# A 31-tap depthwise convolution: its last two channel blocks on TensorE as four stacked, shifted copies and four column groups

## The reference

```python
def mixer_cd(h, w_in, dw_w, dw_b, ln_g, ln_b, sc_w, w_out):
    u = h @ w_in
    v = u[..., :CONF_DIM] * jax.nn.sigmoid(u[..., CONF_DIM:2 * CONF_DIM])
    v = causal_dwconv(v, dw_w) + dw_b            # 31 taps, one filter per channel
    vf = v.astype(jnp.float32)
    mu = jnp.mean(vf, axis=-1, keepdims=True)
    var = jnp.mean(jnp.square(vf - mu), axis=-1, keepdims=True)
    vn = (vf - mu) * lax.rsqrt(var + LN_EPS) * ln_g + ln_b
    conf_out = jax.nn.silu(vn)
    ...                                          # bg * causal_dwconv(cg * hh, sc_w)
    return jnp.concatenate([conf_out, sc_out], axis=-1) @ w_out
```

## Time and profile before

| | us |
|---|---|
| median of three runs | 946.71 (940.55 to 950.35) |
| the profiled execution | 945.4, of which the instructions span 943.7 |
| TensorE busy | 894.6 |
| VectorE busy | 665.2 |
| layer 1's first stage, `gate 0` to the end of `out late` | about 460 to 660 |

### The profile page before, as it was taken

The page is one execution under the profiler, slowest core; times in us unless marked ns, Lnnn a source line. Parts: engine busy times, 40 slices in busy tenths (PEclk is TensorE's granted clock), DMA queues, the critical chain, the costliest instruction groups (busy, mean ns, idle before and its releaser), DMA issues.

```text
span 943.7 us, 17154 instructions
## 1 busy us (share of the span) xinstructions
PE 894.6 (95%) x7268; PEld 869.3 (92%) x7268; DVE 665.2 (70%) x1078; ACT 470.2 (50%) x661; POOL 162.2 (17%) x147
## 2 busy tenths in 40 slices
PE   6999998999999999999999998999989799999997
PEld 6899988998989999999899988889988799999996
DVE  5897996687397555554879999976785485555552
ACT  5544554565465444445643433646574454445443
POOL 1000800000001000000058687457000010000000
PEclk9999999999999999999999999999999899999998
DMA  8454444544555555655645654245541356555551
GB/s 286 141 180 134 136 131 134 180 135 140 169 179 179 184 196 184 192 187 179 182 152 180 193 158 143 80 150 169 178 141 66 132 161 195 192 189 188 191 180 45
DMA packets 81030, 153.73 MB, mean 163 GB/s; under 512 B 6251, under 2 KB 7227, under 8 KB 80955
## 3 DMA queue, kind: packets, MB, share of 16 engines
q1 hardware_dynamic: 80843, 152.60, 50.8%
q10 hardware_dynamic: 112, 0.05, 0.0%
HBM read 151.58 MB, written 1.05 MB: 162 GB/s over the span
## 4 chain that ended last, share of the span: by engine, by line
PE 58%; DVE 29%; ACT 6%; POOL 3%; issue 3%; DMA 1%; DVEq 0%; POOLq 0%
PE ps L495 18%; PE ps L497 18%; PE ps L496 18%; DVE w_lo L1273 8%; DVE ps L1652 6%; ACT w_hi L921 3%; POOL w_lo L1925 2%; DVE E L1444 1%; DVE h_lo L1284 1%; DVE tmp L1587 1%; PE ps L562 1%; DVE xT L1594 1%; DVE E L1452 1%; DVE ml L1886 1%; PE ps L569 1%
## 5 line engine op out<-in xcount | busy, mean ns | idle before, releaser
L921 ACT ACTIVATE w_hi<-raw 128x1024 fp32r<-128x1024 f32 x284 | 295.7, 1054 | 230.0 <-DMA raw<-in_mlp_w 128.4
L495 PE MATMUL ps<-h_hi,w_hi 128*128 128x256 f32 x1280 | 360.6, 282 | 21.2 <-DVE w_lo L1273 8.6
L1273 DVE TENSOR_TENSOR w_lo<-raw,w_hi 128x1024 fp32r<-128x1024 f32 x238 | 291.5, 1247 | 125.4 <-ACT w_hi L921 122.2
L496 PE MATMUL ps<-h_lo,w_hi 128*128 128x256 f32 x1280 | 357.6, 279 | 0.0
L497 PE MATMUL ps<-h_hi,w_lo 128*128 128x256 f32 x1280 | 357.4, 279 | 0.0
L495 PEld LDWEIGHTS ps<-h_hi,w_hi 128*128 128x128 f32 x1280 | 243.6, 190 | 25.8 <-DVE w_lo L1273 11.2
L496 PEld LDWEIGHTS ps<-h_lo,w_hi 128*128 128x128 f32 x1280 | 243.6, 190 | 0.1
L497 PEld LDWEIGHTS ps<-h_hi,w_lo 128*128 128x128 f32 x1280 | 243.6, 190 | 0.0
L495 PE MATMUL ps<-r_hi,w_hi 128*128 128x256 f32 x512 | 144.3, 282 | 0.0
L497 PE MATMUL ps<-r_hi,w_lo 128*128 128x256 f32 x512 | 144.2, 282 | 0.0
L496 PE MATMUL ps<-r_lo,w_hi 128*128 128x256 f32 x512 | 144.1, 281 | 0.0
(11 more groups left out here) (247 smaller groups left out, 1237.1 us busy)
## 6 DMA issues: line engine op xcount, KB each, us to landing
raw<-in_mlp_w SPq DMA_DIRECT2D x128, 512.0 KB, 3.8
raw<-in_cd_w_in SPq DMA_DIRECT2D x40, 512.0 KB, 3.7
raw<-in_xa_wkv SPq DMA_DIRECT2D x32, 512.0 KB, 4.0
raw<-in_ab_w_in SPq DMA_DIRECT2D x24, 512.0 KB, 4.2
raw<-in_xa_wq SPq DMA_DIRECT2D x16, 512.0 KB, 3.8
raw<-in_xa_wo SPq DMA_DIRECT2D x16, 512.0 KB, 3.8
raw<-in_cd_w_out SPq DMA_DIRECT2D x16, 512.0 KB, 3.7
raw<-in_ab_w_out SPq DMA_DIRECT2D x12, 512.0 KB, 3.7
```

The source lines that it names most:

```text
L495: nc.tensor.matmul(dst, wt[0], x[0], start=start, stop=False, skip_group_check=True)
L496: nc.tensor.matmul(dst, wt[0], x[1], start=False, stop=False, skip_group_check=True)
L921: nc.scalar.activation(w_hi[:, v % SLOTS, :, :], raw[:, v % SLOTS, :, :], ACT.Copy)\
L1273: V.tensor_tensor(w_lo[:, v % SLOTS, :, :], raw[:, v % SLOTS, :, :], f(w_hi[:, v % SLOTS, :, :]), ALU.subtract).then_inc(lo_ready_dve, 1)
```

## The change

Blocks 6 and 7 both leave VectorE and the diagonals. Four copies of a group of 32 channels, shifted by 0, 1, 2, 3 tokens, are stacked on the 128 partitions, so one product of K = 128 and 32 output columns does four taps for 32 channels; eight steps do 31 taps (the 32nd is zero), and four channel groups lie in four column groups of the array. That makes 2 blocks x 8 steps x 4 groups = 64 fp32 matmuls with 32 columns of weights and 256 moving columns. The copies are 32 new transfers from `vpad` (32 partitions by up to 284 fp32 each) on SyncE's queue, placed ahead of the load of unit 163 (`hh 0`, fourth unit). Their weights (`quad_w`) are built by one VectorE instruction (128x256) in each of the eight steps of layer 0's MLP. The filter loads become 15 transfers (7 for blocks 0 to 5, 8 for the stacked layout) with their own semaphore, issued after unit 5 and ahead of `poolw` and `memtok`. VectorE's taps end after block 5, at 186.

```diff
+            def dw_inputs():
+                sp_.wait_ge(pool_made, after("pool", "stage0"))
+                for j in range(DVE_BLOCKS):
+                    r0, c = j * KW, slice(j * P, (j + 1) * P)
+                    n0 = min(KW, max(0, P - r0))
+                    if n0:
+                        sp_.dma_start(stage[r0:r0 + n0, 2, :], dw[0:n0, c]).then_inc(dw_landed, 16)
+                    if n0 < KW:
+                        r1 = r0 + n0 - P
+                        sp_.dma_start(stage[r1:r1 + KW - n0, 3, :], dw[n0:KW, c]).then_inc(dw_landed, 16)
+                for m in range(STEPS):
+                    ...
+            def shift_copies():
+                sp_.wait_ge(dve_made, after("dve", "v", 3))
+                sp_.wait_ge(dve_made, after("dve", "shpad"))
+                for b in range(2):
+                    for s_ in range(QUAD):
+                        for g in range(QUAD):
+                            n = min(SHW, KW - 1 + T - s_)
+                            sp_.dma_start(shifted(b)[CQ * s_:CQ * s_ + CQ, g, 0:n],
+                                          vpad[CQ * g:CQ * g + CQ, DVE_BLOCKS + b, s_:s_ + n]).then_inc(shift_landed, 16)
...
                 if u == SLOTS:
+                    dw_inputs()
                     mem_inputs()
+                if u == first[("cg", 0)] + SLOTS + 1:
+                    shift_copies()
                 if u >= SLOTS:
                     sp_.wait_ge(pe_made, after("pe", "unit", u - SLOTS))
...
                     acquire(("conv7",))
-                    pe.wait_ge(dve_made, after("dve", "v", 3))
-                    for k in range(31):
-                        pe.wait_ge(act_made, after("act", "diag", k))
-                        mm = nc.tensor.matmul(bank(("conv7",))[:, 0:T], diag(k), vpad[:, J - 1, k:k + T],
-                                              start=(k == 0), stop=(k == 30))
-                        mm.then_inc(*(finish(("conv7",)) if k == 30 else (pe_made, tick("pe", "tap", k))))
+                    pe.wait_ge(dve_made, after("dve", "quad_w"))
+                    pe.wait_ge(shift_landed, 16 * 2 * QUAD * QUAD)
+                    for b in range(2):
+                        for m in range(STEPS):
+                            for g in range(QUAD):
+                                mm = nc.tensor.matmul(ps[CQ * g:CQ * g + CQ, use[("conv7",)][0], b * T:(b + 1) * T],
+                                                      quad_w[:, 8 * m + QUAD * b + g, :],
+                                                      shifted(b)[:, g, QUAD * m:QUAD * m + T],
+                                                      start=(m == 0), stop=(m == STEPS - 1), skip_group_check=True)
+                    mm.then_inc(*finish(("conv7",)))
...
-                    for k in range(31):
-                        if k >= 4:
-                            act.wait_ge(pe_made, after("pe", "tap", k - 4))
-                        nc.scalar.activation(diag(k), ident[:, :], ACT.Copy, scale=tap(k, J - 1))\
-                            .then_inc(act_made, tick("act", "diag", k))
-                        if k % 8 == 7:
-                            round_to(F_[("out", 1, "early", 0)] + 2 + k // 8)
+                    round_to(F_[("out", 1, "early", 0)] + 3)
                     act.wait_ge(*full(("conv7",)))
-                    nc.scalar.activation(cv[:, J - 1, :], bank(("conv7",))[:, 0:T], ACT.Identity,
-                                         bias=vec("dwb", J - 1)).then_inc(act_made, tick("act", "conv7"))
+                    for b in range(2):
+                        nc.scalar.activation(cv[:, DVE_BLOCKS + b, :], bank2(("conv7",))[:, b, :], ACT.Identity,
+                                             bias=vec("dwb", DVE_BLOCKS + b))\
+                            .then_inc(act_made, tick("act", *(("conv7",) if b else ())))
...
-                    if cur[0] >= 31 * J:
+                    if cur[0] >= KW * DVE_BLOCKS:
                         return
-                    if cur[0] >= 186 and cur[0] % 2:
-                        cur[0] += 1
-                        continue
...
+                        V.tensor_tensor(quad_w[:, 8 * h:8 * h + 8, :],
+                                        vecs[:, QT + 8 * h:QT + 8 * h + 8].unsqueeze(2).broadcast_to([P, 8, CQ]),
+                                        vecs[:, ID32:ID32 + CQ].unsqueeze(1).broadcast_to([P, 8, CQ]), ALU.mult)\
+                            .then_inc(dve_made, tick("dve", *(("quad_w",) if h == STEPS - 1 else ())))
```

More of the change, by code:

```diff
@@ L291, in trunk @@
         h_hi, h_lo = sb("h_hi", [J, T], F32R), sb("h_lo", [J, T], F32R)
+        with ExitStack() as s:
+            quad_w = sb("quad_w", [64, 32], scope=s)
         k_hi, k_lo = sb("k_hi", [J, T], F32R), sb("k_lo", [J, T], F32R)
@@ L338, in trunk @@
             cv, cv3 = sb("cv", [J, T], scope=s), sb("cv3", [J, T], scope=s)
+            with ExitStack() as s2:
+                shift0 = sb("shift0", [4, T + 28], scope=s2)
+                skip((2 * J * T - 4 * (T + 28)) * 4, s2)
+                shift1 = sb("shift1", [4, T + 28], scope=s2)
             mh, ml = sb("mh", [2 * J, T], F32R, s), sb("ml", [2 * J, T], F32R, s)
@@ L360, in trunk @@
                              "out_stored"))
+        dw_landed, shift_landed = sem("dw_landed"), sem("shift_landed")
         raw_landed = [sem(f"raw_landed{i}") for i in range(SLOTS)]
@@ L364, in trunk, with f @@
         pe_made, act_made, dve_made, pool_made = sem("pe_made"), sem("act_made"), sem("dve_made"), sem("pool_made")
+        def f(ap):
+            return ap.bitcast(F32)
         GAIN, MISC, DW = 0, 128, 256
+        dw = A["conf_dw_w"][0]
+        KW = dw.shape[0]
+        DVE_BLOCKS = J - 2
+        QUAD = 4
+        STEPS = (KW + QUAD - 1) // QUAD
+        CQ = P // QUAD
+        SHW = T + QUAD * (STEPS - 1)
+        ID32, QT = GAIN + 96, DW + P + 64
         def gain(l, s, j):
@@ L389, in tap, with shifted @@
         def tap(k, j):
-            return vecs[:, DW + k * J + j:DW + k * J + j + 1]
-        dw_rows = A["conf_dw_w"].rearrange("a k (j p) -> (a k j) p", p=P)
-        DWN = dw_rows.shape[0]
+            at = DW + j * KW + k
+            return vecs[:, at:at + 1]
+        def shifted(b):
+            return (shift0, shift1)[b]
         def bank(label):
@@ L408, in row2 @@
             return r[:, :].unsqueeze(1).broadcast_to([P, 2, T])
-        def f(ap):
-            return ap.bitcast(F32)
         def lo_wait(u):
@@ L448, in later_inputs @@
                     sp_.dma_start(stage[r0:r0 + v.shape[0], 1, :], v).then_inc(vec_landed, 16)
-                sp_.dma_start(stage[:, 2, :], dw_rows[0:P, :]).then_inc(vec_landed, 16)
-                sp_.dma_start(stage[0:DWN - P, 3, :], dw_rows[P:DWN, :]).then_inc(vec_landed, 16)
                 sp_.dma_start(wdt[:, :, :], A["ab_w_in"][0, :, 3072:3088].rearrange("(j p) h -> p j h", p=P))\
@@ L455, in later_inputs @@
                 sp_.dma_start(dall[:, :], A["ssm_d"].broadcast_to([P, HEADS])).then_inc(ssm_landed, 16)
+            def dw_inputs():
[9 more added lines that the diff above has]
+                for m in range(STEPS):
+                    ns = min(QUAD, KW - QUAD * m)
+                    r0 = 64 + 8 * m
+                    sp_.dma_start(stage[r0:r0 + 8, 3, 0:CQ * ns].rearrange("g (s c) -> g s c", c=CQ),
+                                  dw[QUAD * m:QUAD * m + ns, DVE_BLOCKS * P:J * P].rearrange("s (g c) -> g s c", c=CQ))\
+                        .then_inc(dw_landed, 16)
+            def shift_copies():
[7 more added lines that the diff above has]
+                                          vpad[CQ * g:CQ * g + CQ, DVE_BLOCKS + b, s_:s_ + n]).then_inc(shift_landed, 16)
             def mem_inputs():
@@ L600, in _ @@
             rows(("R0",), [rfac[:, 0, t:t + 1] for t in range(TT)])
-            pe.wait_ge(vec_landed, 16 * (2 + len(MISC_ROWS)))
+            pe.wait_ge(vec_landed, 16 * len(MISC_ROWS))
+            pe.wait_ge(dw_landed, 16 * (DVE_BLOCKS + 1 + STEPS))
             transposes(("vecs",), [(P, stage[0:MISC_N, 1, :], MISC_N), (2 * P, stage[:, 2, :], P),
-                                   (3 * P, stage[0:DWN - P, 3, :], DWN - P)])
+                                   (3 * P, stage[:, 3, :], P)])
             pe.wait_ge(dve_made, after("dve", "wdtg"))
@@ L965, in _ @@
             act.wait_ge(*full(("vecs",)))
-            for c, k in ((MISC, MISC_N), (DW, DWN)):
+            for c, k in ((MISC, MISC_N), (DW, 2 * P)):
                 nc.scalar.activation(vecs[:, c:c + k], bank(("vecs",))[:, c:c + k], ACT.Copy)\
@@ L1756, in mlp @@
                     low_to(base + 9)
+                    if l == 0:
+                        if h == 0:
+                            dve.wait_ge(pool_made, after("pool", "id32"))
+                        V.tensor_tensor(quad_w[:, 8 * h:8 * h + 8, :],
+                                        vecs[:, QT + 8 * h:QT + 8 * h + 8].unsqueeze(2).broadcast_to([P, 8, CQ]),
```

(14 more changed lines are left out.)

2 lines of the change are left out of this document (removed).

## The result

| | us |
|---|---|
| changed kernel, median of four | 963.77 (962.15 to 964.97) |
| kernel before, beside it, median of four | 948.53 (940.55 to 953.26) |
| ratio, 95% interval | 1.0178 (1.0143 to 1.0213) |
| profiled execution, its span | 964.12, 962.4 (before 945.4, 943.7) |

The account below looks back on a forecast made before the run. VectorE's taps were taken to bound layer 1's first stage, with TensorE's block 7 and `out early 0` at its end. Terms -9.5 + 10.7 + 0.3 = +1.5 us on the 946.7 median gave 948.2, range 937 to 959.

Parts of the forecast that it names:

- The convolution block: TensorE, block 7's place: 64 matmuls four abreast take 7.3 us; with the wait at `mustat` gone, 9.5 us gained.
- Pacing by issue: Rival at the convolution block: matmuls held to the issue rate, 14.8 us instead of 7.3, 955.7 us in all; chance 0.12.
- The estimate by the Trainium skill: Convolution block: four column tiles at the skill's packing efficiency take 9.2 us, 1.9 more than the sum uses.
- No overlap: Rival at the convolution block: column groups don't overlap four ways, 29.1 us for the matmuls, 970.0 in all; chance 0.08.
- The copies: SyncE's queue ahead of unit 163: 32 issues of 0.352 us take 11.3 us, TensorE stalls 10.0, VectorE runs 10.7 late.
- half clock behind the pause: TensorE at `hh 0` after the copies' stall: 14 records at 1.2 GHz take 3.1 us of the half's 4.3.
- The upper bound: Copies ahead of unit 163: at 0.5 us an issue and the slow clock, VectorE would be 15.5 us late.
- The start: SyncE's queue ahead of unit 6: 15 filter loads for 2 delay `memtok` and unit 6, costing 0.3 us, between 0 and 2.
- The Trainium skill's rule: Filter loads at the start: five loads of 31 rows, a prime, would lie on one engine, making the term 1 to 2 us.
- MLP weights: Layer 0's MLP: eight `quad_w` instructions of some 0.4 us lie beside busy TensorE and cost nothing; without that cover 3.2 us.
- The sum: Whole kernel: block gain -9.5, copies +10.7 and start +0.3 make +1.5 us, forecast 948.2.
- copies at 0.5: Rival ahead of unit 163: dearer copies, up to 0.5 us an issue, make 953.0 us in all; chance 0.09.

Follow-up runs that it names:

- both moves: Changed kernel with its 32 copies spread over seven gaps and the filter loads issued behind units 9 and 11: 937.02 us, ratio to the kernel before 0.9895.
- the execution that kept the full clock: Changed kernel with both channel blocks in one copy, 16 issues at the old place: 953.74 us, ratio to the kernel before 1.0054.

## Why the prediction was wrong

- **The convolution block: right.** Predicted 7.3 us for 64 matmuls, measured 7.11; predicted gain 9.5, measured 9.95, with and without the stalls. `S2` was expected near 606 and `mustat` at 612; with both moves they stand at 606.0 and 610.1, in an execution that reached the block 1.5 us early. Pacing by issue (14.8 us) is refuted by 128 records with their loads in 7.11 us, 0.0555 each. The estimate by the Trainium skill ("TensorE: Matmul & The Clock Gate", Part 3 on packing small matmuls) was 9.2 us; the trace has 7.11. No overlap is refuted, and its price (29.1) was too high: with the groups in turn the block takes 21.98.
- **The copies: mechanism right, one term mis-sized.** "An issue is not free ... I take the mean of six since the copies, too, are many small ones in a line" is the step that failed. The 0.352 us of the earlier trace rows belongs to loads from DRAM; a copy whose source is on the chip took 0.634 from one to the next. 32 x 0.634 = 20.3 instead of 11.3, 9.0 us more. Everything behind that term held: from the load's issue to TensorE 7.7 us (7.4 forecast), TensorE's half to VectorE 4.7 (4.3), half clock behind the pause, all of it passed on. VectorE waited 20.8 us and was 20.5 late by this, where 10.7 stood. The upper bound failed with it: 0.5 was a step among small loads from DRAM, and a bound taken from one kind does not bound another. A few lines further on in the same timeline stood dearer issues that the prediction left out, among them:

```profile
8.14 1.64 SPq L453 DMA_DIRECT2D dtb<-in_ssm_dt_bias  x1
9.82 0.55 SPq L454 DMA_DIRECT2D expA<-in_ssm_a_log  x1
10.42 0.63 SPq L455 DMA_DIRECT2D dall<-in_ssm_d  x1
```

- **The start: wrong in size and in its reason.** Forecast 0.3 (0 to 2), measured 5.2 (about 3 in the execution that kept the full clock) and 1.5 more by a clock fall at 146 us. Its working doesn't give the 0.3 in the first place: unit 6 leaves 2.0 later and lands 1 later still, and of those 3.0 us the row had 0.98 in hand, which leaves 2.0. Two steps failed besides. "At 0.352 an issue" made unit 6 2.0 us late; it was 4.4, since three of the first five filter loads took 0.65, 1.35 and 2.12 us to issue. And "The queue is full of data at that time, so it lands perhaps 1 us later" was wrong: transfers rested at 42 GB/s from 16.5 to 21 while SyncE issued small loads, and then `memtok`'s 1 MB went out 0.55 us ahead of unit 6, where it had been 3.65 us ahead. Unit 6 was rounded 4.6 us later, the row 3.5 later than before, and the slow clock added 1.7 to `dt`.
- **The Trainium skill's rule** on 31 rows ("DMA: Bandwidth & Descriptors", why a DMA increments its semaphore by 16) put this term at 1 to 2 us, nearer than mine but still short. That the line backs up behind four loads of 31 rows would fit it. But the load that was held longest, the fifth in the line (2.12 us, and 1.66 behind unit 9), has only 4 rows, and the last of the five with 31 rows, the seventh in the line, took 0.25. What holds them up, no run here shows.
- **MLP weights: right.** Eight instructions of 0.416 to 0.420 us, nothing of it seen in the units from 84 to 162.
- **The sum.** -9.5 + 10.7 + 0.3 = 1.5 stood there. Measured were 7.2 by unit 162 (5.2 and 1.5, and 0.5 of scatter), 20.5 by the copies, 1.4 by the clock fall ahead of the block and -9.95 at the block, 19.1 in all; the two profiled spans differ by 18.7 (the medians by 15.2). The copies alone would have left the time just inside the range: 948.2 + 9.8 = 958.0. It took the start as well to leave it. The range ended at 959 because it took in one dear case at a time; copies at 0.5 and a start at its upper bound of 2 together would have reached only 954.7, so what failed was the bounds of the terms, not the way they were added.

## What to carry to other kernels

Small transfers ahead of a large one on the same queue cost their issue time, however little data they carry, as soon as the large one is on somebody's path. Count the issues, price them by a row with the same kind of source, and place them where the queue waits for a gate anyway: here the same 32 copies cost 20 us in one piece and nothing in seven gaps. Matmuls with few output columns were worth their packing here only with neighbours in the program going to different column groups; the order of two loops decided between 7.1 and 22.0 us.

## What the runs showed of the hardware

- One issue on SyncE: 0.57 to 0.63 us with a source on the chip, whatever its 8 to 128 rows; 0.42 and 0.47 for the same tile from DRAM; 0.25 to 0.32 for most filter loads.
- Four column groups of 32 overlap: an fp32 matmul of 256 moving columns took 0.111 us with neighbours in the other groups and 0.343 with neighbours in the same group, a ratio of 3.1; one with 128 output columns took 0.455.
- A load of 4 rows behind four loads of 31 rows took 2.12 us to issue in the changed kernel and 1.66 us with the loads moved behind unit 9, while the ten loads behind it took 0.25 to 0.37. The cause was not tried.
- The granted clock fell to 0.50 in a pause of TensorE of 18.8 us and in one of 8.64, and stayed there into the work behind it (17.1 and 10.2 us in all). Two short falls of 3.4 us, near 30 and near 146 us, came in four of five executions with the filter loads ahead of unit 6 and in none of six without; the second lies more than 100 us behind these loads, and how it hangs on them stays open.
